# The sample loop of a hybrid decoder step: the copies are queued behind the values' windows, one of them much later, the next sample's third row is formed earlier, and the softmax is divided after the value product

## The chip, the cores and the metric

One core of a Trainium2 chip runs the whole program. The metric is the device time of one execution in microseconds (us). Engines are named as the profile names them: PE is TensorE (matmul), DVE is VectorE, ACT is ScalarE, POOL is GpSimd, SP is SyncE. SP computes nothing here; it only issues transfers (DMAs).

## The reference, cut to what matters

The program is one inference step of a one-layer decoder for a prompt of 256 tokens and eight samples of 4 new tokens each, with 2048 past positions in each sample's cache. For the change only the samples' part of the first attention counts:

```
# per sample b: 4 queries t, 8 heads h, keys at distances 0, d, 2d.. <= window, for (128,1), (512,4), (2048,16)
logits = einsum('bthd,btjhd->bhtj', q, kg) + bias      # gathered keys
lse    = logsumexp(logits); p = exp(logits - lse)
o      = einsum('bhtj,btjhd->bthd', p, vg)             # merged over the three branches by their sums
...
k_win_sample = k_all[:, n_new:]; v_win_sample = v_all[:, n_new:]   # the caches, moved on by 4 rows
```

The last line means that 2044 of 2048 rows of both caches of each sample are copied from input to output: 8 x 2 caches, each in two pieces of 2044 KB, so 32 copies. They depend on nothing. After the attention follow the output projection, cross-attention over 256 memory tokens, a router and a mixture of 32 experts whose 12 MB of weights each are read once, all in float32.

## The kernel before, in words

All loads and the 32 copies are issued by SP in one written order, and their packets are served in that order. A copy (`copy(n)`, L491, `COPIES`, L276) moves memory to memory and is placed wherever the order has room for it.

**Stages.** (1) Projection of all tokens; the weights `w_in` come in eight chunks (L1505). (2) The sample loop, `b` = 1 to 7 (L1204 on DVE, L1704 on PE, L876 on ACT, L547 on SP). (3) The output projection `out` (L1642, L1628). (4) Cross-attention, which starts with the product `xq` (L1749) and its weights `w_xq`. (5) Router and experts (L1954, L1983), where each expert's weights are loaded as soon as the half before has been used.

**One turn of the sample loop.** The key window of sample b (`window(kwin..)`, 1.75 MB in four transfers, two buffers) must be there; ACT copies its late rows together (`late_keys`, L790, L787). PE spreads each of the four query rows over a bank (`row`, L1564); DVE multiplies it with the keys and sums (`row`, L1163), adds biases and finds the largest score (`largest_score`, semaphore `scored`). POOL reduces that over partitions; in the next turn DVE subtracts (`shift`, L1134), ACT exponentiates (`sample_exp`), DVE and POOL form the sums over all keys (`sums`, L1143; L687), DVE divides (`shares`, L1147), and only then PE multiplies with the values (`values`, L1671). This product also waits for the value window (one buffer) and for `late_values` (L797). DVE masks the product (`keep`, L1153), PE turns it (`turn_values`, L1687) and ACT stores it (`sample_out`, L861). Beside this each turn carries one unit of the prompt's attention (`logits`, `share`, `turned`, `unit_values`) and long products of 16 matmuls (`fill`, L1648): `mk` twice in turns 1 and 2, with `w_xk`; `mv` once in turns 3 to 6, with `w_xv`.

**What sets the order.** PE's products rotate over seven banks in the order of `jobs` (L254 to L341): `take` waits until the product seven places before has been read. SP's order in a turn (L547 to L558): wait for `scored` b, key window b+1, then `w_xv` (turn 3), `w_out` (turn 7) or copies, then wait until the value product b-1 is full (L1682 is its last matmul), value window b. A transfer behind such a wait is not issued before it ends.

Of the kernel before, what the change touches and what calls it, by code (L numbers as in the profile page):

```python
# [8 lines left out]
P = 128  # L9
# [43 lines left out]
def constants():  # L53
# [22 lines left out]
    col = np.arange(AW)  # L76
    own = ((p[:, None] // 32 == p[:, None] // 8 % 4) & (p[:, None] % 8 == col[None, :] // HD)).astype(np.float32)
    diag = np.concatenate([own, (p[:, None] // 32 == np.arange(DEC_T)[None, :]).astype(np.float32)], 1)
# [20 lines left out]
def build(nc, i, o):  # L99
# [5 lines left out]
    with ctx:  # L105
# [86 lines left out]
        zs = small[:, 320:352]  # L192
        zz = small[:, 352:384]
        stat = small[:, 384:440]

        own = hn[:, 2, 0:AW + DEC_T]
# [79 lines left out]
        COPIES = [5, 1, 3, 1, 2, 2, 2, 2, 2, 2, 3, 2, 1, 3]  # L276
# [30 lines left out]

        add("pt", DEC_B - 1)
        add("pvt", DEC_B - 2), add("o", DEC_B - 1), add("out", 0, 0), add("out", 0, 1), add("pv", DEC_B - 1)
# [99 lines left out]
        zpart = sem("zpart")  # L409
        zall = sem("zall")  # L410
        prob = sem("prob")
# [56 lines left out]

        block = ctx.enter_context(nc.Block())
# [3 lines left out]
        def _(sp):  # L473
            load(sp, "ident", ident[:, :], i["c_ident"])
            for t in (0, 2, 1):
# [71 lines left out]
            for b in range(1, DEC_B):  # L547
# [105 lines left out]
        def _(pool):  # L653
# [23 lines left out]
            for b in range(DEC_B):  # L677
# [8 lines left out]
                pool.wait_ge(zpart, b + 1)  # L686
                nc.gpsimd.partition_all_reduce(zz, zs, P, bass.bass_isa.ReduceOp.add).then_inc(zall, 1)  # L687
# [60 lines left out]
        def _(act):  # L748
# [12 lines left out]

            act.wait_ge(consts, 2)
# [97 lines left out]

            def sample_out(b):  # L861
# [14 lines left out]
            for b in range(1, DEC_B):  # L876
                unit_pt(b - 1)
                if b >= 2:
                    sample_out(b - 2)
# [4 lines left out]
                unit_out(b - 1)  # L884
                unit_exp(b)
# [4 lines left out]
            unit_pt(DEC_B - 1)  # L890
            sample_out(DEC_B - 2)
            unit_out(DEC_B - 1)
            late_values(DEC_B - 1)
            sample_exp(DEC_B - 1)
# [3 lines left out]
            for t, (t0, n) in enumerate(TOK):  # L898
                if t == 1:
                    sample_out(DEC_B - 1)  # L900
# [109 lines left out]
        def _(dve):  # L1010
# [132 lines left out]
            def sums(b):  # L1143
                dve.wait_ge(sexp, b + 1)
                V.tensor_reduce(zs, pr[:, :, :, :].rearrange("p k t h -> p (t h) k"), AX.X, ALU.add).then_inc(zpart, 1)

            def shares(b):  # L1147
                dve.wait_ge(zall, b + 1)
                link(V.reciprocal(zz, zz))
                V.tensor_tensor(pr[:, :, :, :].rearrange("p k t h -> p k (t h)"), pr[:, :, :, :].rearrange("p k t h -> p k (t h)"),  # L1150
                                zz.unsqueeze(1).broadcast_to([P, 4, 32]), ALU.mult).then_inc(prob, 1)

            def keep(b):  # L1153

                if b:
                    b_, use = place(("pvt", b - 1))
                    dve.wait_ge(bank_full[b_], use + 1)
                else:
                    dve.wait_ge(loaded["diag"], 16)
                ps, s = product(dve, "pv", b)  # L1160
                V.tensor_tensor(kept, ps[:, :], own[:, 0:AW], ALU.mult).then_inc(s, 1)

            def row(b, t):  # L1163
# [3 lines left out]
                if b:  # L1167
                    pair = kw[:, 0:8, :].rearrange("p (k s) n -> p k s n", k=2)[:, :, t, :]
                    V.tensor_tensor(pd[:, 0:2, :], pair, ps[:, :].unsqueeze(1).broadcast_to([P, 2, AW]), ALU.mult)  # L1169
                    V.tensor_tensor(pd[:, 2, :], kw[:, 8, :], ps[:, :], ALU.mult).then_inc(s, 1)  # L1170
                else:
                    V.tensor_tensor(pd[:, 0, :], near_first[:, t, :], ps[:, :], ALU.mult)
                    V.tensor_tensor(pd[:, 1, :], far_first[:, t, :], ps[:, :], ALU.mult)
                    V.tensor_tensor(pd[:, 2, :], late_first, ps[:, :], ALU.mult).then_inc(s, 1)
# [17 lines left out]
            dve.wait_ge(late_k, 1)  # L1192
# [8 lines left out]
            dve.wait_ge(late_k, 2)  # L1201
            row(1, 0), shift(0)
            logits(0)
            for b in range(1, DEC_B):  # L1204
# [4 lines left out]
                dve.wait_ge(late_k, b + 1)  # L1209
                for t in range(0 if b > 1 else 1, DEC_T):  # L1210
# [13 lines left out]
            shift(DEC_B - 1), keep(DEC_B - 2), sums(DEC_B - 1), shares(DEC_B - 1)  # L1224
# [25 lines left out]
            for t, (t0, n) in enumerate(TOK):  # L1250
                residual("out", t)
                if t == 0:
                    keep(DEC_B - 1)
# [208 lines left out]
        def _(pe):  # L1462
# [28 lines left out]
            pe.wait_ge(rb_rep, 1)  # L1491
            for kind in range(6):
# [5 lines left out]
            ps, s = take(pe, "toep")  # L1498
            M(ps[0:HEADS, 0:TOEP], rb, cb[:, 0:TOEP], start=True, stop=True).then_inc(s, 1)
# [171 lines left out]
            def values(b):  # L1671
                pe.wait_ge(prob, b + 1)
# [365 lines left out]
```

## Time and profile before

| | |
|---|---|
| median of 3 runs | 1409.87 us (1401.8 to 1410.43) |
| the profiled execution | 1409.75 us, span 1408.0 us |
| PE busy, DVE busy, ACT busy | 1255.7 us (89%), 481.2 us (34%), 230.3 us (16%) |
| moved by DMA | 557.14 MB, mean 396 GB/s |
| chain that ended last | DMA 55%, PE 35%, DVE 5%, ACT 2% |
| largest piece of the chain | DMA wide<-in_w_gate_up, 49% |

The page cuts the span into 40 slices and gives for each the busy share of every engine in tenths. The chain follows the last instruction back through whatever released it. The rows below come from it and from closer questions: busy time by stretch, the order of instructions of one engine in time, and the chain piece by piece. In a timeline, the bracket gives the idle time before the instruction and what ended it.

### The profile page before, as it was taken

To read this page: it belongs to the slowest core of one execution; us is meant where nothing else is said; L and a number is where in the kernel's file an instruction comes from. 1 tells how busy PE (TensorE), PEld (TensorE's weight loads), DVE (VectorE), ACT (ScalarE), POOL (GpSimd) and SP (SyncE) were. 2 spreads that over 40 slices of the span, in tenths; PEclk is the share of its full clock that TensorE was granted. 3 is DMA by queue.
4 is the path that set the end of the run, shared out by engine and by line. 5 is a ranking of instruction groups with operands and counts; after the bars stand their busy time and mean duration, and the time that the engine had idled before them with its cause. 6 is when DMAs were issued, how large, how long until landed. Compare 5 with 4: busy or idle time off the path is not lost.

```text
span 1408.0 us, 16530 instructions
## 1 busy us (share of the span) xinstructions
PE 1255.7 (89%) x6407; PEld 528.5 (38%) x6407; DVE 481.2 (34%) x1037; ACT 230.3 (16%) x448; POOL 67.7 (5%) x69
## 2 busy tenths in 40 slices
PE   7989877989897999998999989999899998999986
PEld 5444323456644433333333333333333333333332
DVE  2387888332326412312232122321223212132124
ACT  1334443211311110110110100110011010011102
POOL 2010000005007000000000000000000000000000
PEclk9999988999997999999999999999999999999998
DMA  9999999998989699999999999999999999999993
GB/s 339 353 381 363 399 397 379 361 370 306 360 354 344 254 431 427 427 429 426 429 428 429 429 429 429 428 430 427 430 427 430 427 429 428 429 429 429 429 428 158
DMA packets 51740, 557.14 MB, mean 396 GB/s; under 512 B 7021, under 2 KB 9301, under 8 KB 15885
## 3 DMA queue, kind: packets, MB, share of 16 engines
q1 hardware_dynamic: 50629, 553.04, 96.0%
q0 software_dynamic: 1072, 3.57, 0.6%
q8 instruction: 26, 0.43, 0.1%
q14 instruction: 13, 0.11, 0.0%
HBM read 552.02 MB, written 71.72 MB: 443 GB/s over the span
## 4 chain that ended last, share of the span: by engine, by line
DMA 55%; PE 35%; DVE 5%; ACT 2%; issue 1%; SPq 1%; DVEq 0%; ACTq 0%; PEldq 0%
DMA wide<-in_w_gate_up 49%; PE bank L1954 12%; DMA wide<-in_cache_v_win 3%; PE bank L1642 3%; PE bank L1983 2%; PE bank L1684 2%; PE bank L1749 2%; PE bank L1512 2%; PE bank L1508 1%; PE bank L1662 1%; DMA slim<-in_w_xq 1%; DMA slim<-in_w_xv 1%; ACT wide L787 1%; PE bank L1737 1%; PE bank L1791 1%
## 5 line engine op out<-in xcount | busy, mean ns | idle before, releaser
L1954 PE MATMUL bank<-wide,att 128*64 128x512 f32 x2048 | 463.3, 596 | 58.5 <-DMA wide<-in_w_gate_up 58.3
L1954 PEld LDWEIGHTS bank<-wide,att 128*64 128x64 f32 x2048 | 139.3, 136 | 362.5 <-issue 228.8
L1983 PE MATMUL bank<-slim,att 128*64 128x512 f32 x1024 | 226.8, 595 | 0.0
L1422 DVE TENSOR_SCALAR att<-bank 128x512 f32<-128x512 f32 x32 | 22.1, 691 | 469.0 <-PE bank L1954 469.0
L1983 PEld LDWEIGHTS bank<-slim,att 128*64 128x64 f32 x1024 | 70.6, 137 | 152.2 <-issue 149.2
L1401 DVE TENSOR_TENSOR x<-x,bank 128x512 f32<-128x512 f32 x68 | 46.6, 685 | 233.1 <-PE bank L1936 226.4
L980 ACT ACTIVATE att<-att 128x512 f32<-128x512 f32 x32 | 20.2, 630 | 517.6 <-DVE att L1422 517.6
L1936 PE MATMUL bank<-tb,att 128*128 128x512 f32 (+1 forms) x192 | 84.7, 611 | 1.8 <-ACT tb L989 1.3
L989 ACT ACTIVATE tb<-bank 64x512 f32<-64x512 f32 x64 | 37.8, 591 | 234.1 <-PE bank L1983 233.7
L1662 PE MATMUL bank<-slim,ta 128*128 128x512 f32 x128 | 57.8, 601 | 0.5 <-DMA slim<-in_w_xv 0.3
L1176 DVE TENSOR_REDUCE small<-wide 128x24 f32<-128x1536 f32 x28 | 49.1, 1753 | 1.0
L1684 PE MATMUL bank<-wide,pr 128*32 128x512 f32 x192 | 33.0, 840 | 17.5 <-ACT wide L787 11.4
L1903 PE MATMUL bank<-att,mkT 128*128 128x128 bf16 x408 | 46.3, 223 | 1.4 <-DVE att L1352 1.4
L1903 PE MATMUL bank<-att,ta 128*128 128x128 bf16 x408 | 45.7, 222 | 0.0
L787 ACT ACTIVATE wide<-wide 32x512 f32<-32x512 f32 x60 | 37.6, 626 | 44.3 <-DMA wide<-in_cache_v_win 24.5
L1169 DVE TENSOR_TENSOR wide<-wide,bank 128x1024 f32<-128x1024 f32 x28 | 33.9, 1210 | 6.0 <-PE bank L1568 3.9
L1662 PEld LDWEIGHTS bank<-slim,ta 128*128 128x128 f32 x128 | 23.4, 190 | 33.4 <-issue 29.7
L1903 PEld LDWEIGHTS bank<-att,mkT 128*128 128x128 bf16 x408 | 28.3, 99 | 15.2 <-issue 14.6
L1749 PE MATMUL bank<-ta,slim 128*128 128x288 f32 x128 | 31.6, 408 | 2.7 <-DMA slim<-in_w_xq 1.8
L1429 DVE TENSOR_TENSOR att<-att 128x512 f32<-128x512 f32 x32 | 33.4, 1044 | 1.1
L985 ACT ACTIVATE att<-bank 128x512 f32<-128x512 f32 x32 | 19.1, 597 | 74.9 <-PE bank L1974 74.9
L1974 PE MATMUL bank<-ident,att 128*128 128x128 f32 x128 | 21.0, 286 | 11.5 <-DVE att L1429 9.6
(290 smaller groups left out, 1153.1 us busy)
## 6 DMA issues: line engine op xcount, KB each, us to landing
wide<-in_w_gate_up SPq DMA_DIRECT2D x128, 2048.0 KB, 25.4
slim<-in_w_down SPq DMA_DIRECT2D x64, 2048.0 KB, 22.0
out_k_win_sample<-in_cache_k_win SPq DMA_DIRECT2D x16, 2044.0 KB, 25.3
out_v_win_sample<-in_cache_v_win SPq DMA_DIRECT2D x16, 2044.0 KB, 22.9
wide<-in_w_in SPq DMA_DIRECT2D x8, 1024.0 KB, 15.8
wide<-in_cache_v_win SPq DMA_DIRECT2D x8, 1024.0 KB, 7.5
wide<-in_cache_mem_k SPq DMA_DIRECT2D x8, 1024.0 KB, 24.4
wide<-in_cache_mem_v SPq DMA_DIRECT2D x8, 1024.0 KB, 14.7
```

The lines of the kernel that those rows point to most:

```text
L787: ins = A(late[32 * s:32 * s + 32, :], win[96:128, s, :], ACT.Copy)
L989: ins = A(ye[i // 2][CAP * (i % 2):CAP * (i % 2) + CAP, 512 * h:512 * h + 512], bank_y[CAP * h:CAP * h + CAP, :], ACT.Copy)
L1176: link(V.tensor_reduce(S_[b % 2][:, :, t, :], pd.rearrange("p k (h d) -> p k h d", d=HD), AX.X, ALU.add))
L1401: ins = V.tensor_tensor(dst, dst, bk[:, :], ALU.add)
L1642: ins = M(tk[h][0][0:n, :], left[:, k, t0:t0 + n], slim[:, k, 512 * h:512 * h + 512], start=k == 0, stop=k == KC - 1)
L1662: ins = M(ps[:, :], ta[:, k, P * t:P * t + P], slim[:, k, 512 * h:512 * h + 512], start=k == 0, stop=k == KC - 1)
L1684: ins = M(ps[g, :], flat[:, kind, :], vwin[:, 8 if kind == 2 else 4 * kind + t, :], start=k == 0, stop=False)
L1749: ins = M(ps[:, 0:T], slim[:, k, P * c:P * c + P], ta[:, k, :], start=k == 0, stop=k == KC - 1)
L1903: M(bk[:, c:c + 2 * CAP], hparts[t][:, s, P * k:P * k + P], onehot[:, t, :], start=t == 0 and s == 0, stop=False)
L1936: ins = M(out, back[buf][:, t0:t0 + m], ye[buf][:, 512 * h:512 * h + 512], start=True, stop=True)
L1954: ins = M(bk[half[h], :], rows[:, k, :], wide[:, k, c:c + 512], start=False, stop=k == KC - 1)
L1983: ins = M(bank_y[half[h], :], aT[:, f % 4, f // 4, :], slim[:, f, 512 * h:512 * h + 512], start=f == 0, stop=f == KC - 1)
```

## The change

- SP: `COPIES` has 4 instead of 5 copies in front, 2 instead of 1 before the router's late loads, 2 instead of 3 behind expert 0's first weights, and so 2 instead of 1 remain for the end of that place. In the sample loop the copies of a turn are issued behind the value window instead of ahead of it.
- `ident` and the prompt's second tile are loaded from ACT's queue; the 0/1 matrix `own` has 32 columns instead of 516. PE forms the product `toep` ahead of the ten small bias products.
- `row(b + 1, 2)` moves on PE from the start of turn b+1 to just behind `values(b - 1)`, ahead of the long product; `turn_values(b - 2)` moves behind `unit_values`.
- DVE's `sums` and `shares`, POOL's second reduce and the semaphores `zpart`, `zall`, `prob` go. `values` multiplies the undivided exponentials, and 16 matmuls of one column give the sums per row; DVE inverts them (`part_of_sum`), ACT divides while it reads the product (`keep`, now on ACT). The masking falls to `turn_values`, which has 8 matmuls instead of 4.
- DVE waits for the late keys only at the third product of row 0, PE for the late values only at their matmuls.

```
-        COPIES = [5, 1, 3, 1, 2, 2, 2, 2, 2, 2, 3, 2, 1, 3]
+        COPIES = [4, 1, 3, 1, 2, 2, 2, 2, 2, 2, 3, 2, 2, 2]
...
-            add("qb", b, 2), add("pt", b - 1)
+            if b == 1:
+                add("qb", b, 2)
+            add("pt", b - 1)
+            for f in FILL[b, 0]:
+                add(*f)
+            add("qb", b, 3), add("o", b - 1)
             if b >= 2:
                 add("pvt", b - 2)
-            for f in FILL[b, 0]:
-                add(*f)
-            add("qb", b, 3), add("o", b - 1), add("s", b, 0), add("s", b, 1)
+            add("s", b, 0), add("s", b, 1)
             if b + 1 < DEC_B:
                 add("qb", b + 1, 0), add("qb", b + 1, 1)
             add("pv", b - 1)
+            if b + 1 < DEC_B:
+                add("qb", b + 1, 2)
...
                 if b in ROUND_AT:
                     slim_round(ROUND_AT[b])
-                else:
-                    copy(COPIES.pop(0))
 
                 bb, use = place(("pv", b - 1))
                 sp.wait_ge(bank_full[bb], use + 1)
                 window(vwin, i["cache_v_win"], b, v_in)
+                if b not in ROUND_AT:
+                    copy(COPIES.pop(0))
...
+            load(act, "ident", ident[:, :], ident_rows)
+            load(act, "x1", x[:, 1, :], second_rows)
...
+            def keep(b):
+                if b:
+                    b_, use = place(("pvt", b - 1))
+                    act.wait_ge(bank_full[b_], use + 1)
+                act.wait_ge(rz_in, b + 1)
+                ps, s = product(act, "pv", b)
+                A(kept, ps[:, :], ACT.Copy, scale=rz[:, b:b + 1]).then_inc(s, 1)
...
                 unit_pt(b - 1)
                 if b >= 2:
-                    sample_out(b - 2)
+                    keep(b - 2)
                 sample_exp(b - 1)
                 late_values(b - 1)
...
                 unit_out(b - 1)
+                if b >= 2:
+                    sample_out(b - 2)
...
+            def part_of_sum(b):
+
+                b_, use = place(("pv", b))
+                dve.wait_ge(bank_full[b_], use + 1)
+                V.reciprocal(rz[:, b:b + 1], sx_bank[:, b:b + 1]).then_inc(rz_in, 1)
...
-                    if t < 3:
-                        (shift, sums, shares)[t](b - 1)
-                    if b >= 2 and t == 0:
-                        keep(b - 2)
+                    if t == 0 and b > 1:
+                        shift(b - 1)
+                        part_of_sum(b - 2)
...
             def values(b):
-                pe.wait_ge(prob, b + 1)
+                pe.wait_ge(sexp, b + 1)
+                pe.wait_ge(rz_in, b)
                 pe.wait_ge(v_in, 64 * (b + 1))
-                pe.wait_ge(late_v, b + 1)
...
-                for k, kind in enumerate((2, 0, 1, 3)):
+                for kind in range(4):
+                    for t in range(DEC_T):
+                        n = NS if kind == 3 else P
+                        M(sx_bank[32 * t:32 * t + 32, b:b + 1], flat[0:n, kind, :], ones[0:n, 0:1], start=kind == 0, stop=kind == 3,
+                          tile_position=(0, 32 * t))
+                for k, kind in enumerate((0, 1, 2, 3)):
+                    if kind == 2:
+                        pe.wait_ge(late_v, b + 1)
```

## Rows read from the trace of the kernel before

**Rows 1.** The page, 40 slices of 35.2 us: share of the DMA engines, what they moved.
```profile
DMA  9999999998989699999999999999999999999993
GB/s 339 353 381 363 399 397 379 361 370 306 360 354 344 254 431 427 427 429 426 429 428 429 429 429 429 428 430 427 430 427 430 427 429 428 429 429 429 429 428 158
```
**Rows 2.** Busy time by stretch: length, PE, PEld, DVE, ACT, POOL, PEclk, DMA share, GB/s.
```profile
121.00:146.00 25.00, 20.95 (x83) 9.48 (x86) 20.03 (x34) 8.54 (x19) 1.39 (x3) 0.88 1.00 365
190.00:252.00 62.00, 47.77 (x228) 20.11 (x226) 54.67 (x82) 20.94 (x47) 2.89 (x6) 0.83 0.96 368
...
250.00:252.00 2.00, 2.00 (x20) 1.04 (x16) 1.40 (x4) 0.00 (x0) 0.14 (x1) 1.00 0.09 35
...
386.00:399.00 13.00, 12.35 (x99) 6.89 (x99) 2.77 (x4) 1.15 (x3) 0.00 (x0) 0.88 0.68 262
...
454.00:469.00 15.00, 11.15 (x89) 7.52 (x90) 8.80 (x50) 0.95 (x6) 0.00 (x0) 0.77 0.16 54
...
507.00:1360.00 853.00, 786.74 (x4117) 282.82 (x4117) 204.34 (x450) 86.25 (x140) 0.00 (x0) 1.00 1.01 428
```
**Rows 3.** SP's queue in order of time, sample loop: start, duration, transfer.
```profile
120.42 0.33 SPq L512 DMA_DIRECT2D wide<-in_cache_v_win  x1
...
148.23 0.34 SPq L512 DMA_DIRECT2D wide<-in_cache_v_win  x1
...
188.85 0.33 SPq L512 DMA_DIRECT2D wide<-in_cache_v_win  x1
...
209.73 0.33 SPq L512 DMA_DIRECT2D wide<-in_cache_v_win  x1
...
251.24 0.33 SPq L512 DMA_DIRECT2D wide<-in_cache_v_win  x1
```
**Rows 4.** ACT in order of time: the copies of late rows that start with a window's landing.
```profile
138.73 2.54 ACT L787 ACTIVATE wide<-wide 32x512 f32<-32x512 f32 x4 [8.98 <-DMA wide<-in_cache_v_win]
200.89 2.54 ACT L787 ACTIVATE wide<-wide 32x512 f32<-32x512 f32 x4 [3.16 <-DMA wide<-in_cache_v_win]
205.20 2.54 ACT L787 ACTIVATE wide<-wide 32x512 f32<-32x512 f32 x4 [0.32 <-DMA wide<-in_cache_k_win]
221.75 2.54 ACT L787 ACTIVATE wide<-wide 32x512 f32<-32x512 f32 x4 [2.70 <-DMA wide<-in_cache_v_win]
...
258.57 2.54 ACT L787 ACTIVATE wide<-wide 32x512 f32<-32x512 f32 x4 [4.53 <-DMA wide<-in_cache_v_win]
```
**Rows 5.** PE in order of time, front: the second tile's transposes, the first projection matmuls.
```profile
9.53 1.97 PE L1486 MATMUL bank<-ident,x 128*128 128x128 f32 x8 [2.55 <-DMA x<-in_x_prompt]
...
17.72 4.18 PE L1508 MATMUL bank<-ta,wide 128*128 128x288 f32 x8 [0.77 <-ACT att L775]
```
**Rows 6.** DVE in order of time, turn 6: first product of row 0, `keep`, `sums`.
```profile
208.84 1.21 DVE L1169 TENSOR_TENSOR wide<-wide,bank 128x1024 f32<-128x1024 f32 x1
...
213.03 0.69 DVE L1161 TENSOR_TENSOR wide<-bank,hn 128x512 f32<-128x512 f32 x1 [0.21 <-DVE pp L1139]
...
219.15 0.38 DVE L1145 TENSOR_REDUCE small<-pr 128x32 f32<-128x128 f32 x1 [1.92 <-ACT pr L859]
```
**Rows 7.** PE in order of time: small products, a long product, value products, first of `xq`.
```profile
71.25 0.84 PE L1560 MATMUL bank<-att 64*32 64x32 f32 x16 [1.51 <-ACT att L805]
...
120.29 7.13 PE L1662 MATMUL bank<-slim,ta 128*128 128x512 f32 x16
...
203.68 4.99 PE L1684 MATMUL bank<-wide,pr 128*32 128x512 f32 x24 [3.09 <-ACT wide L787]
...
268.03 2.78 PE L1684 MATMUL bank<-wide,pr 128*32 128x512 f32 x24
...
302.29 1.71 PE L1749 MATMUL bank<-ta,slim 128*128 128x288 f32 x6 [0.90 <-DVE ta L1046]
```
**Rows 8.** The chain that ended last, in order of time: start, duration, what.
```profile
158.53 14.80 DMA slim<-in_w_xv
...
290.67 15.09 DMA slim<-in_w_xq
```

More of the change, by code:

```diff
@@ L191, in build @@
         gm = small[:, 288:320]
-        zs = small[:, 320:352]
-        zz = small[:, 352:384]
+        rz = small[:, 320:320 + DEC_B]
         stat = small[:, 384:440]
-        own = hn[:, 2, 0:AW + DEC_T]
+        own = hn[:, 2, 0:HEADS * DEC_T]
         kept = wf[:, 15360:15872]
@@ L473, in _ @@
         def _(sp):
-            load(sp, "ident", ident[:, :], i["c_ident"])
-            for t in (0, 2, 1):
+            for t in (0, 2):
                 t0, n = TOK[t]
@@ L890, in _ @@
             unit_pt(DEC_B - 1)
+            unit_out(DEC_B - 1)
+            keep(DEC_B - 2)
+            sample_exp(DEC_B - 1)
+            late_values(DEC_B - 1)
             sample_out(DEC_B - 2)
-            unit_out(DEC_B - 1)
-            late_values(DEC_B - 1)
-            sample_exp(DEC_B - 1)
             act.wait_ge(stored["mk"], 16)
@@ L899, in _ @@
                 if t == 1:
+                    keep(DEC_B - 1)
                     sample_out(DEC_B - 1)
@@ L1141, in shift @@
                 dve.sem_inc(shifted, 1)
[L1143 to L1161, printed above, removed]
+            def part_of_sum(b):
+                b_, use = place(("pv", b))
+                dve.wait_ge(bank_full[b_], use + 1)
+                V.reciprocal(rz[:, b:b + 1], sx_bank[:, b:b + 1]).then_inc(rz_in, 1)
             def row(b, t):
@@ L1223, in _ @@
             share(DEC_B - 1, DEC_B, P * (UNITS[DEC_B - 1][1] + 1))
-            shift(DEC_B - 1), keep(DEC_B - 2), sums(DEC_B - 1), shares(DEC_B - 1)
+            shift(DEC_B - 1), part_of_sum(DEC_B - 2)
             for u in range(2):
@@ L1252, in _ @@
                 if t == 0:
-                    keep(DEC_B - 1)
+                    part_of_sum(DEC_B - 1)
                 norm(5 + t, n, x[0:n, t, :], hn[0:n, t, :], 6 + t)
@@ L1491, in _ @@
             pe.wait_ge(rb_rep, 1)
+            ps, s = take(pe, "toep")
+            M(ps[0:HEADS, 0:TOEP], rb, cb[:, 0:TOEP], start=True, stop=True).then_inc(s, 1)
             for kind in range(6):
@@ L1690, in turn_values @@
                 ps, s = take(pe, "pvt", b)
-                for c in range(4):
-                    ins = M(ps[:, 4 * c:4 * c + 4], kept[:, P * c:P * c + P], own[:, AW:AW + DEC_T], start=True, stop=True)
+                if b == 0:
+                    pe.wait_ge(loaded["diag"], 16)
+                for h in range(HEADS):
+                    ins = M(ps[64 * (h % 2):64 * (h % 2) + 64, 4 * (h // 2):4 * (h // 2) + 4], kept[:, HD * h:HD * h + HD],
+                            own[:, DEC_T * h:DEC_T * h + DEC_T], start=True, stop=True)
                 ins.then_inc(s, 1)
@@ L1704, in _ @@
             for b in range(1, DEC_B):
-                row(b, 2)
+                if b == 1:
+                    row(b, 2)
                 turned(b - 1)
-                if b >= 2:
-                    turn_values(b - 2)
                 for f in FILL[b, 0]:
@@ L1712, in _ @@
                 unit_values(b - 1)
+                if b >= 2:
+                    turn_values(b - 2)
                 scores(b)
@@ L1716, in _ @@
                 values(b - 1)
+                if b + 1 < DEC_B:
+                    row(b + 1, 2)
                 for f in FILL[b, 1]:
@@ L1719, in _ @@
             turned(DEC_B - 1)
-            turn_values(DEC_B - 2)
             unit_values(DEC_B - 1)
@@ L1724, in _ @@
             rows_times("out", 0, tb, P, 0)
+            turn_values(DEC_B - 2)
             values(DEC_B - 1)
```

23 lines of the change are left out of this document (9 added, 14 removed).

## The prediction

> **What bounds the kernel now.** I read the slices of the page first: the DMA engines are busy in nearly every slice [rows 1]. By stretch they are full in turns 1 and 2 of the sample loop, nearly full in the later turns and all through the experts [rows 2]; the idle spots are 250 to 252 us, 386 to 399 (0.32 x 13 = 4.2 us) and 454 to 469 (0.84 x 15 = 12.6 us). So up to the weights of `xq` the end is set by bytes in SP's order plus whatever time that queue stands empty. SP's order next [rows 3]: value windows are issued at 120.42, 148.23, 188.85, 209.73 and 251.24; the 20.9 us from the third to the fourth are one steady turn. Landings are read from ACT [rows 4]. The last window met an empty queue and landed after 258.57 - 251.24 = 7.3 us. A window alone takes 205.20 - 200.89 = 4.3 us, so about 3.0 us are issue and completion. Between 205.20 and 221.75 lie one window and two copies: a **copy** costs (16.55 - 4.3) / 2 = 6.1 us. A turn of two windows and two copies is 20.8 us, which is the turn seen: the loop runs at the pace of the queue. Value window 1 landed after 18.3 us, so 11.0 us of other work lay ahead of it. That backlog is what kept the queue full while PE did the two long products of turn 2.
>
> **The change, part by part.**
>
> *Front.* PE waited 2.55 us for the second tile and 0.77 us for ACT's copy of `toep` [rows 5]; the new loads and the new order attack both. Bounds 0 and 3.3; I take 2.5, since other loads (gains, bias) are due at about the same time. PE's front then leads by 2.5 us. The Trainium skill (DMA: Bandwidth & Descriptors, section Issuing engines are not separate DMA queues) says that starting a transfer from another engine saves only the time to start it; by that rule the tile would gain about 1 us and the front 1.8.
>
> *Softmax divided late.* Gone from DVE per turn: the wait ahead of `sums` (1.92), `sums` (0.3 net), `shares` (two small operations, about 0.6 by the size of `sums`) and `keep` (0.6 and a gap of 0.2) [rows 6]; added a reciprocal (0.2). DVE's turn falls by 3.3 us from the 20.9 of the queue that it follows; worth nothing as long as the queue sets the pace. Gone from POOL one reduction, hidden. Added on PE 16 matmuls, 32 records, of 32 columns of weights and one of data. Not in the trace: bounds 0 (beside others) and 3.8 us (long weights); the nearest row is 16 small records in 0.84 us [rows 7], or 52 ns each, 1.7 us; I take 2.0, twice that at the low clock. The Trainium skill (TensorE: Matmul & The Clock Gate, section LDWEIGHTS) lets the load time follow the number of columns alone; its 27 ns for 32 columns would make an estimate of 0.9 us. `turn_values` with 16 records instead of 8: 0 to 0.8 us, hidden by PE's slack in turns 4 to 6. `keep` on ACT (0.7) stands ahead of `sample_exp` and `late_values`, and it waits for `part_of_sum` on DVE, behind row 0; PE's `turn_values` and scores wait for it. PE is ahead of DVE there, so 0.
>
> *Banks.* With the third row and `turn_values` moved, the bank of `values(b - 1)` is the one of `row(b, 3)`, seven places before. So the value product can't start before DVE has multiplied row 3: row 0 and `shift` 4.2 us, rows 1 and 2 at 3.5 each (219.15 - 1.92 - 213.72), and by the 1.21 of a product of two thirds about 1.9 for row 3's products and 1.3 for `logits`, together 14.4 us after DVE's turn began [rows 6]. That is what `prob` cost before, so the wait is replaced, not removed. The third row ahead of the long product takes 0.3 us from it and hides nothing, as DVE reaches row 2 later than either place. The late waits save 1.2 us on DVE and about 2 on PE, hidden in the same way.
>
> *Copies, place by place.* One copy fewer in front and turn 1's one behind value window 1: 12.2 us fewer ahead of it against 11.0 us of backlog. The queue reaches it empty.
>
> Gap A. Value window 1 is issued near 120 (front -2.5, new matmuls +2.0). Then come 4.3 + 6.1 + 4.3 = 14.7 us of work (window, copy, key window 3), and SP stands at its wait for value product 1. PE needs two long products (14.1), the row sums (2.0), the product (2.8 and 1.0) and some eight small groups like the one of 0.84, less what lies side by side, an estimate of 5.5: 25.5; before, the interval was 27.8. Empty for 11 us (9 to 13).
>
> Value window 2 is then issued at 145.5. Ahead of the end of `w_xv` lie the window 4.3, two copies 12.2, key window 4.3 and `w_xv` itself, 4.19 MB at the 428 GB/s of the experts [rows 2], 9.8; with 3.0 for completion it lands at 179.1, against 158.53 + 14.80 = 173.3 before [rows 8]. `mv` waits for it.
>
> Gap B. From that landing to the next value window's issue passed 188.85 - 173.3 = 15.5 us, filled by two windows and copies. Now only the two windows (8.6) are issued before that wait, as turn 3 has no copies. Empty for 15.5 + 3.0 - 8.6 = 10, less the store of `mem_k` (2.5) which falls here or just before; I take 7 (5 to 10).
>
> Gap C. Value window 4 goes out at 194.6, then two copies, then key window 6, which lands at 194.6 + 4.3 + 12.2 + 4.3 + 3.0 = 218.4. DVE's turn 6 begins there; it began at 208.84 before. Value product 5 starts 1.4 (late keys) + 14.4 later and takes 5.8 to 8, so it is full at 240 to 242, while the queue ran out after 4.3 + 12.2 + 4.3 of turn 5, at 237. Empty for 4 (0 to 9). What was late before was the value window; what is late now is the **key window behind two copies**.
>
> *The end of it.* Empty time 11 + 7 + 4 = 22 us; before, 250 to 252 cost 1.8 and its edges 0.5. One copy fewer ahead of `w_xq` is -6.1. So `w_xq` lands 22 - 2.3 - 6.1 = **13.6 us later**. PE was ready for `xq` at 302.29 [rows 7] and went on at 290.67 + 15.09 = 305.8: 3.5 us of cover, and PE's own path moves by less than the weights do, so all 13.6 count. From there to the experts PE and DVE set the pace, and the shift is carried.
>
> *The late copies.* Two copies instead of one after 386: 6.1 us into 4.2 of idle, so expert 0's weights come 2 us later; they are first used when the router is done, near the end of the idle stretch 454 to 469, and that leaves them slack. The one moved behind `w_down` goes into those 12.6 us; if that idle time were used up, expert 1's weights would start later by the overflow, at most 1 us. 0.
>
> **Sum.** 1409.75 (the profiled execution, next to the median 1409.87) + 13.6 = **1423 us**. With the low ends of the gaps (14) it is +5.6, with the high ends (32) +23.6.
>
> **Rivals.**
> 1. *The queue stays fed; the moved copy is the gain.* If the value product is full much sooner (PE never waits, its clock stays up) the gaps A and C shrink to the 2.3 us there were, and gap B disappears behind the store and early issue. Then the copy taken to 386 us is worth 6.1 and the gap at 250 another 2.3: 1401.4. It decides if the gaps sum to under 8.4 us. For it: DVE loses 3.3 us a turn and PE's waits for `late_values` go. Against it: gap A stands on two long products that nothing shortens.
> 2. *The clock falls at each value product.* A value product after 3.09 us of idle PE took 4.99 us, one right behind other matmuls 2.78 [rows 7], and PEclk was 0.83 in these turns against 1.00 later. With more waiting in turns 2, 3, 5 and 6 each adds 1.5 us for the sums and 1 for the product: +10 on the chain, 1433. The Trainium skill (TensorE: Matmul & The Clock Gate, section HAM oscillation) says that a matrix engine which waits for transfers restarts at 1.2 GHz; the trace agrees.
> 3. *Nothing on balance.* The gaps come to 8 to 13 us because stores and the order hide part: 1408 to 1414.
>
> **How the numbers follow.** The forecast case (+6 to +19) has 0.50, rival 1 0.13, rival 2 0.20, rival 3 0.17. About 1% (14 us) is what can be told from no change here. Slower by more than that: 0.22 of the forecast case, all of rival 2: 0.42. Faster by more: only a tail of rival 1, 0.03. The rest is 0.55. The range runs from rival 1 to just over rival 2, 1402 to 1435.
>
> **What would show it.** Right: value window 1 lands within 8 us of its issue; the DMA share falls well under 1.00 between 135 and 146 and again behind `w_xv`; `w_xv` lands near 179; ACT's copy for key window 6 starts near 218; `w_xq` lands near 319; DVE's turns wait for key windows. Wrong: a DMA share of 1.00 through 121 to 146, or a loop turn of under 20 us with both windows early. If `w_xq` comes later but the experts start no later, the carrying was wrong.

## The result, and the profile after

| | before | after |
|---|---|---|
| median, same chip and hour | 1408.09 us (1401.8 to 1410.43, 4 runs) | 1431.49 us (1429.98 to 1432.42, 4 runs) |
| ratio | 1 | 1.0178, 95% interval 1.0149 to 1.0207 |
| profiled execution, span | 1409.75, 1408.0 | 1429.98, 1428.2 |
| chain: DMA, PE | 55%, 35% | 54%, 36% |

The change costs 23.4 us by the medians and 25 by the ratio. The forecast was 1423 in a range of 1402 to 1435, a change of 13.6: the direction, the place and the mechanism are right, the size is about 10 us short. The measured time lies nearer to the 1433 of rival 2 than to 1423; why that rival is not the cause stands below, with the other rivals.

The page of after, cut into 40 slices like [rows 1]: the digits 8, 7 and 8 in the fourth, sixth and seventh slice of the DMA line are holes that were not there.

```profile
DMA  9998978999999799999999999999999999999993
GB/s 354 347 358 291 338 278 309 382 377 365 334 324 395 304 402 427 428 427 426 430 427 428 430 427 430 429 427 429 429 427 431 427 427 430 428 427 431 427 427 161
```

After by stretch; the last three numbers are the granted clock, the share of the DMA engines and GB/s, as in [rows 2]. The first row reaches from 83 us, near the first key window of the turns, to where `xq` gets its last weights.

```profile
83.00:328.40 245.40, 198.27 (x1159) 89.92 (x1158) 146.85 (x227) 83.85 (x184) 8.02 (x14) 0.85 0.89 336
121.00:146.00 25.00, 22.66 (x136) 9.93 (x135) 21.00 (x30) 9.10 (x19) 1.28 (x2) 0.93 0.60 236
146.00:190.00 44.00, 31.68 (x182) 13.90 (x180) 25.56 (x36) 14.41 (x30) 1.01 (x2) 0.81 0.99 381
190.00:200.00 10.00, 7.96 (x67) 2.38 (x68) 9.62 (x16) 4.04 (x11) 0.43 (x1) 0.66 0.02 6
190.00:252.00 62.00, 48.08 (x308) 19.15 (x309) 44.35 (x64) 20.53 (x47) 1.30 (x3) 0.78 0.75 276
```

The same stretch in the kernel before:

```profile
83.00:305.80 222.80, 187.62 (x847) 85.97 (x845) 160.87 (x254) 79.02 (x176) 11.71 (x22) 0.92 0.99 381
```

Length times (1 - share) gives the time without transfers: 245.4 x 0.11 = 27.0 us after, 222.8 x 0.01 = 2.2 before (each 1.2 either way, as the share has two digits). Length times share is the time with them: 218.4 and 220.6. So the whole of the 22.6 us by which `xq` is later is time in which the transfer engines stood still: 24.8 us more of it, and 2.2 less of transfers.

SP's queue after (answers to [rows 3]): the first key window of the turns (83.26 before), value windows 1 and 2, the weights `w_xv`, value window 4 with the two copies and the key window that now follow it, and value window 6:

```profile
80.09 0.33 SPq L513 DMA_DIRECT2D wide<-in_cache_k_win  x1
...
119.69 0.33 SPq L513 DMA_DIRECT2D wide<-in_cache_v_win  x1
...
145.10 0.33 SPq L513 DMA_DIRECT2D wide<-in_cache_v_win  x1
...
152.26 15.35 SPq L509 DMA_DIRECT2D slim<-in_w_xv  x8
...
199.10 0.33 SPq L513 DMA_DIRECT2D wide<-in_cache_v_win  x1
...
201.29 0.63 SPq L495 DMA_DIRECT2D out_v_win_sample<-in_cache_v_win  x1
201.96 0.60 SPq L495 DMA_DIRECT2D out_k_win_sample<-in_cache_k_win  x1
202.60 0.60 SPq L513 DMA_DIRECT2D wide<-in_cache_k_win  x1
...
247.25 0.33 SPq L513 DMA_DIRECT2D wide<-in_cache_v_win  x1
```

ACT after, at the start of turn 6 ([rows 4] before), and DVE there ([rows 6] before): both wait for the key window that stands behind two copies.

```profile
224.80 2.54 ACT L788 ACTIVATE wide<-wide 32x512 f32<-32x512 f32 x4 [12.74 <-DMA wide<-in_cache_k_win]
```

```profile
224.80 1.22 DVE L1168 TENSOR_TENSOR wide<-wide,bank 128x1024 f32<-128x1024 f32 x1 [8.97 <-DMA wide<-in_cache_k_win]
```

PE after ([rows 7] before): row sums (L1680) and value product (L1690) of turns 2, 4 and 7, between them the long product that waited for `w_xv`, and `xq`. L1171 is the second instruction of a row's product on DVE, over the last third of its key rows:

```profile
139.10 0.54 PE L1680 MATMUL bank<-ones,pr 128*32 128x1 f32 x32 [2.34 <-DVE wide L1171]
139.57 4.48 PE L1690 MATMUL bank<-wide,pr 128*32 128x512 f32 x24
...
173.05 5.91 PE L1661 MATMUL bank<-slim,ta 128*128 128x512 f32 x8 [7.31 <-DMA slim<-in_w_xv]
...
192.04 0.71 PE L1680 MATMUL bank<-ones,pr 128*32 128x1 f32 x32 [2.34 <-DVE wide L1171]
192.68 5.35 PE L1690 MATMUL bank<-wide,pr 128*32 128x512 f32 x24
...
257.21 0.54 PE L1680 MATMUL bank<-ones,pr 128*32 128x1 f32 x32
257.68 2.78 PE L1690 MATMUL bank<-wide,pr 128*32 128x512 f32 x24
...
328.40 11.79 PE L1761 MATMUL bank<-ta,slim 128*128 128x288 f32 x35 [1.23 <-DMA slim<-in_w_xq]
```

The chain after, its transfers up to `xq` ([rows 8] before). A key window is on it now.

```profile
162.54 20.84 DMA slim<-in_w_xv
...
204.57 20.21 DMA wide<-in_cache_k_win
...
267.44 18.68 DMA wide<-in_cache_v_win
...
309.46 18.90 DMA slim<-in_w_xq
```

From `xq` to the experts the shift is carried almost whole: 22.6 us there, 19.75 at the first weights of expert 1 (issued at 467.00 before, 486.75 after), 20.2 in the span.

### The profile page after: what moved, and what is told of

Read it like the earlier page. It is cut to its first block, busy times and chain, and to the rows that moved or that the text cites. A ratio compares the mean times of both kernels' runs of the same rounds, so it can differ in the third digit from the quotient of the medians.

```text
span 1428.2 us, 17140 instructions
## 1 busy us (share of the span) xinstructions
PE 1268.1 (89%) x6727; PEld 533.1 (37%) x6727; DVE 469.4 (33%) x1013; ACT 235.2 (16%) x456; POOL 64.3 (5%) x61
## 4 chain that ended last, share of the span: by engine, by line
DMA 54%; PE 36%; DVE 6%; SPq 2%; issue 1%; ACT 1%; DVEq 0%; PEldq 0%; ACTq 0%
DMA wide<-in_w_gate_up 48%; PE bank L1966 12%; PE bank L1661 2%; PE bank L1995 2%; PE bank L1761 2%; PE bank L1641 2%; PE bank L1690 2%; PE bank L1511 1%; DMA slim<-in_w_xv 1%; PE bank L1573 1%; DMA wide<-in_cache_k_win 1%; DMA slim<-in_w_xq 1%; DMA wide<-in_cache_v_win 1%; PE bank L1507 1%; PE bank L1749 1%
## 5 line engine op out<-in xcount | busy, mean ns | idle before, releaser
L993 ACT ACTIVATE att<-att 128x512 f32<-128x512 f32 x32 | 20.2, 631 | 517.9 <-DVE att L1421 517.9
L1761 PE MATMUL bank<-ta,slim 128*128 128x288 f32 x128 | 36.8, 451 | 5.7 <-DMA slim<-in_w_xq 5.7
L1690 PE MATMUL bank<-wide,pr 128*32 128x512 f32 x192 | 33.8, 855 | 0.0
L1761 PEld LDWEIGHTS bank<-ta,slim 128*128 128x128 f32 x128 | 26.6, 211 | 15.6 <-DMA slim<-in_w_xq 5.9
## 6 DMA issues: line engine op xcount, KB each, us to landing
wide<-in_w_gate_up SPq DMA_DIRECT2D x128, 2048.0 KB, 25.5
```

Of the source, the lines that this page charges most:

```text
L1690: ins = M(ps[g, :], flat[:, kind, :], vwin[:, 8 if kind == 2 else 4 * kind + t, :], start=k == 0, stop=False)
L1761: ins = M(ps[:, 0:T], slim[:, k, P * c:P * c + P], ta[:, k, :], start=k == 0, stop=k == KC - 1)
```

## The experiments

Two theories at the start. **S**: SP's order is the cause; with the copies behind the value window, nothing is left to transfer while SP waits for the value product. **C**: the order of the computation is, with a value product that waits for the third row and meets a low clock. Each time below is a median with the kernel before run beside it on the same chip; that kernel gave 1405.5, 1407.1 and 1406.7 us in the three sets, single runs from 1399.9 to 1413.7. One profiled execution therefore stands up to 7 us off its median, and differences of a few us are read from the medians. Profiles of kernels with the same front differ before any of the moved work is reached: in the nine profiles with the whole new front PE begins the first projection product between 12.49 and 15.48 us (14.92 after; 12.65, 12.49 and 12.83 in experiments 1, 6 and 8). Some 2 us of a difference between two `xq` times can be that. "`xq` goes at" is the time at which PE had its last weights or operands for `xq` in the profile (305.8 before, 328.4 after).

**1. Copies ahead again.** In the changed kernel:

```
                 if b in ROUND_AT:
                     slim_round(ROUND_AT[b])
+                else:
+                    copy(COPIES.pop(0))
                 bb, use = place(("pv", b - 1))
                 sp.wait_ge(bank_full[bb], use + 1)
                 window(vwin, i["cache_v_win"], b, v_in)
-                if b not in ROUND_AT:
-                    copy(COPIES.pop(0))
```

> The changed kernel with one part undone: in the sample loop the copies stand ahead of the value window again, as in the kernel before; everything else of the change stays. Theory S (the order on SyncE's queue costs it: with the copies behind the values the transfer engines stand empty for about 10, 10 and 4.5 us at 136, 190 and 244 us): the empty stretches go, the weights w_xq land 6 to 9 us ahead of the kernel before (which landed them at 307.0), and the time is 1400 to 1406 us. Theory C (the order of the computation costs it: each value product is held by DVE's product of the third row of the next sample, and runs at the low clock): the time stays at 1420 us or more.

1402.63 us (10 runs), ratio to before 0.9988 (0.9961 to 1.0015); `xq` goes at 297.8. By stretch:

```profile
83.00:297.80 214.80, 186.81 (x1153) 85.98 (x1151) 143.94 (x225) 83.41 (x184) 7.46 (x14) 0.90 1.00 379
121.00:146.00 25.00, 21.57 (x131) 9.19 (x130) 19.98 (x31) 8.76 (x19) 0.43 (x1) 0.86 0.98 373
190.00:200.00 10.00, 6.60 (x76) 3.39 (x78) 7.92 (x11) 5.95 (x15) 0.00 (x0) 0.82 1.03 428
```

One part undone takes back the whole loss, 27 us by the ratios and 29 by the medians, and the holes with it: 0.60 becomes 0.98, 0.02 becomes 1.03. Theory C falls: the clock was 0.86 in these 25 us, lower than the 0.93 after, and it did not matter.

**2. The counts alone.** Changed kernel, `COPIES` of before (five in front), copies behind.

```
-        COPIES = [4, 1, 3, 1, 2, 2, 2, 2, 2, 2, 3, 2, 2, 2]
+        COPIES = [5, 1, 3, 1, 2, 2, 2, 2, 2, 2, 3, 2, 1, 3]
```

> The changed kernel with only the counts of the copies of before (five at the front and one in the last place, for four and two); the copies stay behind the values. Theory S: the fifth copy at the front is moved out of full stretches only, so 0 to 3 us come back or are lost: 1426 to 1433 us. If the count mattered more than the order, the time would fall to 1415 us or less.

1434.85 us (4 runs), ratio 1.0218 (1.0173 to 1.0262); `xq` goes at 330.7. The time is 1.9 us above what was expected at most. Moving one copy away from the front gave the changed kernel 2.3 us at `xq`, 3.4 by the medians and 5.6 by the ratios. The two intervals overlap, so this doesn't tell the 6.1 of the forecast from less.

**3. The order alone.** Kernel before, and in it:

```
                     slim_round(ROUND_AT[b])
-                else:
-                    copy(COPIES.pop(0))
...
                 window(vwin, i["cache_v_win"], b, v_in)
+                if b not in ROUND_AT:
+                    copy(COPIES.pop(0))
```

> The kernel before with one part of the change alone: in the sample loop each copy stands behind the value window. Softmax, row order, counts and front are those of before. Theory S: the time rises by 12 to 19 us, to 1420 to 1427 us, with empty stretches of the transfer engines ahead of value windows 2, 4 and 6. Theory C: at most 1411 us.

1427.61 us (4 runs), 0.6 above the expected range, ratio 1.0148 (1.0106 to 1.0191); `xq` goes at 320.2.

```profile
83.00:320.20 237.20, 194.29 (x845) 86.34 (x843) 160.24 (x253) 79.34 (x176) 11.76 (x22) 0.89 0.94 356
121.00:146.00 25.00, 25.00 (x106) 11.21 (x105) 22.28 (x35) 8.65 (x19) 1.39 (x3) 1.00 0.83 311
190.00:200.00 10.00, 10.00 (x40) 3.55 (x33) 9.54 (x15) 2.14 (x4) 0.43 (x1) 0.93 0.55 206
```

A move of one statement, with not a byte and not an instruction more, makes 21 of the 25 us (by the ratios 0.0148 and 0.0178) of the whole change. It does so at a granted clock of 1.00 in the stretch with the first hole, so a slow PE is no condition for it.

**4. The old queue under the new computation.** Changed kernel, the edit of experiment 1 and

```
-        COPIES = [4, 1, 3, 1, 2, 2, 2, 2, 2, 2, 3, 2, 2, 2]
+        COPIES = [5, 1, 3, 1, 2, 2, 2, 2, 2, 2, 3, 2, 1, 3]
```

> The changed kernel with SyncE's order and counts of the sample loop both as before; softmax divided late, the third row early, and the first loads on ACT stay. Theory S: within 3 us of the kernel before, 1405 to 1411 us. Theory C: 1420 us or more. Beside the first kernel of this set it gives what the one copy moved from the front is worth: some 4 us against it, if full stretches carry a moved copy one for one.

1406.65 us (10 runs), ratio 0.9992 (0.9969 to 1.0014); `xq` goes at 299.9. Against experiment 1 the moved copy shows 4.0 us by the medians, but 0.6 by the ratios, and the single runs of both reach from 1398 to 1407.5 and more; the 2.1 us at `xq` are no more than the 1.9 by which this profile began its first projection product later (14.56 for 12.65). So its worth is not shown here. Late division, early third row and new front together are worth nothing that can be told at the end.

**5. The third row back.** Changed kernel, in the list of PE's work:

```
-            if b == 1:
-                add("qb", b, 2)
-            add("pt", b - 1)
+            add("qb", b, 2), add("pt", b - 1)
...
-            if b + 1 < DEC_B:
-                add("qb", b + 1, 2)
```

> The changed kernel with one part undone: the product of row 2 of the next sample stands ahead of the scores' transposition again, as before; copies stay behind the values. Forecast's step on the gate (the value product waits until DVE has taken row 3 out of the bank, whichever row stands first, because the same banks turn round): if the early third row is what makes the value windows 1, 2 and 4 late, the empty stretches shrink to those of the kernel with only the order changed (share of the transfer engines .83 at 121:146) and xq is let go at about 320 us instead of 328; time 1423 to 1428 us. If it is the late division that makes them late, nothing moves: 1430 to 1434 us, xq at 326 to 330.

1433.47 us (2 runs), ratio 1.0191 (1.0147 to 1.0235); `xq` goes at 327.0, 121:146 has a share of 0.61. Nothing moves beyond the noise, so the early third row is not what makes the holes longer than in experiment 3.

**6. One copy ahead, one behind.** Changed kernel, where turn 1 has its only copy ahead:

```
                     slim_round(ROUND_AT[b])
+                else:
+                    copy(1)
+                    COPIES[0] -= 1
```

> The changed kernel with one copy of each turn ahead of the value window and the other behind it. A copy occupies the transfer engines for some 6 us. Theory S: each gap is filled by 6 us of its 10, 10 and 4.5, so xq is let go at 309 to 314 us (328.4 after, 297.8 with all copies ahead) and the time is 1411 to 1417 us. If the loss were all or nothing (one late value window shifts all that follows), it stays above 1423 us.

1411.09 us (8 runs), ratio 1.0025 (1.0008 to 1.0043); `xq` goes at 308.1, 0.9 us below the expected range.

```profile
83.00:308.10 225.10, 191.67 (x1153) 87.03 (x1151) 144.59 (x225) 83.48 (x184) 7.46 (x14) 0.88 0.95 362
121.00:146.00 25.00, 21.75 (x131) 9.19 (x130) 20.02 (x31) 8.77 (x19) 0.43 (x1) 0.86 0.78 298
190.00:200.00 10.00, 9.68 (x38) 3.83 (x30) 9.50 (x11) 0.94 (x3) 0.00 (x0) 0.99 0.72 278
```

The price is graded: `xq` at 328.4, 308.1, 297.8 with none, one or all of a turn's copies ahead, and 0.11, 0.05 and 0.00 of the stretch without transfers. The first copy brings back 20 us (of which some 2 may be the earlier start of this profile) and the second 10, as the first fills 6 us of each hole and the holes were only 10, 10 and 4 long. It is bytes in the hole that count, not whether a window is late.

**7. Two copies from ahead of `w_xq` to the end.** Experiment 1 with

```
-        COPIES = [4, 1, 3, 1, 2, 2, 2, 2, 2, 2, 3, 2, 2, 2]
+        COPIES = [4, 1, 3, 1, 2, 2, 2, 2, 2, 0, 3, 2, 2, 2]
```

> The kernel with all copies ahead of the values (first of the set before) with two copies more taken from the place just ahead of the weights w_xq and put last, behind step 0 of the experts, where the transfer engines stand empty for about 10 us ahead of step 1 in every kernel of this study. If the time is set by how full the transfer engines are up to step 1, w_xq lands some 8 us earlier (289 to 291 us), the last copies cost nothing, and the time is 1390 to 1396 us. Rival: the chain through the computation from xq to the experts is not shortened, or the two copies delay step 1 by their 12 us; then it stays at 1400 to 1406 us.

1400.68 us (10 runs), ratio to before 0.9966 (0.9941 to 0.9991): the rival of the expectation. The weights are no longer what `xq` waits for; DVE is:

```profile
295.62 9.69 PE L1761 MATMUL bank<-ta,slim 128*128 128x288 f32 x32 [2.24 <-DVE ta L1059]
```

So `xq` goes 2.2 us earlier than in experiment 1 instead of 8 (about 4 if the 1.9 us by which this profile began later are taken off), and 34 x 0.23 = 7.8 of the 12 us of transfers moved away became a hole in the place they left, where experiment 1 has a share of 1.00:

```profile
252.00:286.00 34.00, 33.38 (x198) 14.70 (x197) 8.06 (x22) 7.73 (x14) 0.00 (x0) 1.00 0.77 298
```

**8. Turns without copies.** Changed kernel with

```
-        COPIES = [4, 1, 3, 1, 2, 2, 2, 2, 2, 2, 3, 2, 2, 2]
+        COPIES = [4, 1, 3, 0, 0, 0, 0, 0, 0, 0, 3, 2, 2, 2]
```

All 32 copies are still made, 15 of them behind step 0.

> The changed kernel with all 13 copies of the turns and of the place ahead of w_xq moved behind step 0. No copy stands ahead of or behind a value window, so what is left is what the turns take by their computation and windows alone. Theory S: value window b is then issued when its product lets it, w_xq is let go at 275 to 285 us, and a turn is near 20 us. Theory C (the order of the computation is itself slower): w_xq is not let go before 300 us. The time itself is worse for the 13 copies now standing in one place: 13 x 6.1 = 79 us, less 10 to 15 of empty time, less what the turns gain (15 to 25 against the kernel before): 1440 to 1465 us.

1473.77 us (1 run). SP's value windows 3, 4, 5 and 6:

```profile
163.32 0.33 SPq L513 DMA_DIRECT2D wide<-in_cache_v_win  x1
...
184.19 0.33 SPq L513 DMA_DIRECT2D wide<-in_cache_v_win  x1
...
204.27 0.33 SPq L513 DMA_DIRECT2D wide<-in_cache_v_win  x1
...
224.44 0.33 SPq L513 DMA_DIRECT2D wide<-in_cache_v_win  x1
```

With no copies in the queue the turns from value window 4 on take 20.1 and 20.2 us. Experiment 1, the same computation with two copies a turn ahead of the wait, issues these windows at 184.80, 204.86 and 225.03: 20.1 and 20.2 as well. So the copies were free there, and the computation alone sets this pace. Against the 20.9 of [rows 3] in the kernel before that is at most 0.8 us a turn for DVE's relief, and none of it shows in the time (experiment 4). `w_xq` was issued at 282.6, inside the 275 to 285 expected, but `xq` went only at 297.0, as DVE's operand was not ready: the earlier weights gained nothing. The time is 9 us above my range for the same reason, and because a copy costs more than 6.1 us: 75.3 us more than the execution of experiment 1 (1398.46), plus some 10 us that stood empty there at 440 to 456, is 85 us for 13 copies, an estimate of 6.6 each.

**9. Order and the two loads.** The edits of experiments 3 and 10 in the kernel before, of which the second is

```
+            load(act, "ident", ident[:, :], ident_rows)
+            load(act, "x1", x[:, 1, :], second_rows)
```

> The kernel before with two parts of the change: the copies behind the value windows, and the identity matrix and the second rows of the prompt loaded from ACT's queue. Division, row order and counts are those of before. With the order alone xq was let go at 320 us, with the late division and this front besides at 327. If the late division is what makes up the difference, this kernel lets xq go at 316 to 320 us and takes 1422 to 1428 us. If the earlier start of the windows only makes the empty stretch behind them longer and shifts the rest, it lets xq go at 324 us or later: 1430 us or more.

1430.14 us (4 runs), ratio 1.0175 (1.0156 to 1.0195); `xq` goes at 321.7, between the two theories. The median is 2.5 us above experiment 3 and 4.7 below experiment 2 (which has the late division and the new PE order besides, with the same five copies in front). With intervals of this width the times only say that neither part is large. The traces say more of the first hole. With the two loads the share of 121:146 falls from 0.83 to 0.67: the earlier front makes the hole longer. And from value window 1 to value window 2 pass 21.4 us here and in experiment 3, but 25.2 to 26.7 in after and experiments 2 and 5, the kernels that have the late division and the copies behind.

**10. The two loads alone.** Kernel before with them.

```
-            load(sp, "ident", ident[:, :], i["c_ident"])
-            for t in (0, 2, 1):
+            for t in (0, 2):
...
+            load(act, "ident", ident[:, :], ident_rows)
+            load(act, "x1", x[:, 1, :], second_rows)
```

> The kernel before with the new front alone (the identity matrix and the second rows loaded from ACT's queue). Forecast's step: the first key window of the turns is issued some 3 us earlier (80.1 against 83.3 us) and, the transfer engines being full from there to w_xq, all of it reaches the end: 2.5 us less than the kernel before, ratio .998. Rival: it is lost on the way, ratio 1.000.

1404.00 us (12 runs), ratio 0.9982 (0.9966 to 0.9997), 2.5 us by the ratio (0.4 to 4.8): as forecast. `xq` goes at 302.1, 3.7 us earlier than before. Where the queue is fed, a front that is earlier comes through; behind a hole (experiment 9 against 3) it does not.

**11. Copies ahead and the third row back.** The edits of experiments 1 and 5 in the changed kernel, of which the second is

```
-            if b == 1:
-                add("qb", b, 2)
-            add("pt", b - 1)
+            add("qb", b, 2), add("pt", b - 1)
```

> The kernel with all copies ahead of the values, with the product of row 2 back in its old place, so only the late division, the front and the counts of the change are left. Forecast's step: the early third row hides nothing, so the same time as with it: 1400 to 1406 us, ratio to that kernel within .3%. If the early third row is worth what fills TensorE's wait ahead of the long product (3.1 us a turn before), xq starts 6 us or more later.

1402.03 us (10 runs), ratio 0.9971 (0.9954 to 0.9988), against 1402.63 with the early third row. No worth of it can be told, with the holes or without.

**12. Kernel before, two copies last.**

```
-        COPIES = [5, 1, 3, 1, 2, 2, 2, 2, 2, 2, 3, 2, 1, 3]
+        COPIES = [5, 1, 3, 1, 2, 2, 2, 2, 2, 0, 3, 2, 1, 3]
```

> The kernel before with the two copies that stand just ahead of w_xq put last, behind step 0 of the experts, and nothing else. Before, xq waited for w_xq from 290.7 to 305.8 us while 456 to 467 us stood empty. w_xq is then bound by its own issue (287.9 us) and its transfer: landed at 298 to 300 us, 6 to 8 us earlier, and the last copies fit into the empty stretch: 1398 to 1402 us, ratio .993 to .996. Rival: as with the two copies last in the kernel with the late division (1400.7 for 1402.6), nearly nothing comes through: ratio .998 or above.

1403.12 us (12 runs), ratio 0.9978 (0.9967 to 0.9989). Half of what was expected:

```profile
302.17 31.28 PE L1749 MATMUL bank<-ta,slim 128*128 128x288 f32 x128 [0.87 <-DVE ta L1046]
```

`xq` goes at 302.2 for 305.8. The forecast had read the cover right (3.5 us, from PE ready at 302.29 in [rows 7]), and I did not use it here: of weights that come about 8 us earlier only those 3.5 count.

## Why the forecast was right, and where it was short

*Copies, the decisive step: right.* "What was late before was the value window; what is late now is the key window behind two copies": DVE waited 8.97 us for key window 6. (It waited 9.56 for key window 4 too, at 171.70, which the forecast left out; there `w_xv` came later still and set the time.) Experiments 1 and 3, each one statement, switch the loss off and on. Value window 2 was forecast at 145.5 and issued at 145.10.

*The three holes.* Read from after:

| | forecast | after |
|---|---|---|
| A | 11 (9 to 13) | 25.00 x 0.40 = 10.0 |
| B | 7 (5 to 10) | 10.00 x 0.98 = 9.8 |
| C | 4 (0 to 9) | 244 to 250: 6 x 0.71 = 4.3 |
| elsewhere | 0 | 27.0 less these three: 2.9 (1.2 either way) |

*Gap A: right in the sum, by luck in the parts.* From value window 1 to 2 the forecast had 25.5 us and the trace has 25.4. But it had 5.5 for the small groups and 2.0 for the row sums, where the trace has some 3.3 and 0.5; and it had no wait and a value product at full clock, where PE waited 2.34 us for DVE and the product took 4.48 instead of 2.78. This wait is the one that the forecast called replaced; in experiment 3, with the old division, PE had none there and the product at 137.86 took 2.78. So with the copies behind, the late division, with the order on PE that comes with it, costs 4.0 us of this interval (21.4 in experiments 3 and 9).

**Gap B** was put too small. The forecast took 2.5 us off for the store of `mem_k`, "which falls here or just before". It fell before: between 144 and 185 us the trace of after has 14.80 MB, 1.05 of them this store. POOL issued it at 161.98 us; in the kernel before, where the turn's second reduce stood ahead of it on POOL, at 178.86, and in experiment 9 at 185.09. So it filled no hole and stood ahead of `w_xv`, which PE had at 183.4 instead of the forecast's 179.1, and value window 4 followed at 199.10 for 194.6. In experiment 9, with the store behind that stretch, `w_xv` was there at 179.6. The store can explain 2.5 of the 4.3 us by which `w_xv` was late, an estimate from its bytes; the rest I can't name. From `w_xv` to that value window passed 15.7 us, forecast 15.5.

*Key window 6* landed 25.7 us after value window 4 was issued, forecast 23.8. Two copies at the 6.6 of experiment 8 in place of 6.1 would make 1.0 of it.

*"One copy fewer ahead of `w_xq` is -6.1": right in bytes, not in time; the largest miss.* In the stretch to `xq` 245.4 x 336 = 82.5 MB were moved for 84.9 before, and 2.4 MB are 6.2 us at the rate of before. But the time with transfers fell by only 2.2 us, as the busy engines moved 378 GB/s for 385. The two digits of the share leave 2 GB/s to rounding on either side, so up to 4 of these 7. The lower rate isn't tied to the holes, as experiment 1 had 379 without any; its cause stays open.

Together: empty time +24.8 for +19.7, transfers -2.2 for -6.1, which is 22.6 for 13.6. Of the 9.0 us missing at `xq`, 3.9 are the moved copy, 2.8 gap B and 2.9 the small empty spots outside the three gaps, which the forecast had at nothing (1.0 of them at 83 to 98, a share of 0.93 where before had 1.00); gap A takes 1.0 off.

*Front: right.* PE's wait for the second tile is gone, the first key window of the turns was issued at 80.09 for 83.26, and the loads alone are worth 2.5 us in experiment 10. Over all profiles PE begins the first projection product at 16.93 to 17.72 us with the old front (3 kernels), at 15.54 and 16.04 with the loads alone, and at 12.49 to 15.48 with the whole new front (9 kernels, the middle one 14.56): about 1.5 us for the loads and 2.7 for all, forecast 2.5. The wait of 0.77 us for ACT's copy of `toep` is still there with the loads alone and gone with PE's new order, which no run took by itself; the rest is within the spread of single profiles. By the rule of the Trainium skill (DMA: Bandwidth & Descriptors, Issuing engines are not separate DMA queues) I had about 1 us for the tile and 1.8 for the front, both somewhat below what the profiles show; that only the time to issue is saved, no run here shows or refutes.

*Row sums: too dear.* 32 records in 0.54 us at a granted clock of 1.00 and 0.71 at 0.50, forecast 2.0. The estimate from the Trainium skill (TensorE: Matmul & The Clock Gate, LDWEIGHTS) was 0.9, also too high, but here it was the better guide than the row of 16 small records in 0.84 us.

*Banks: right in place.* PE waits 2.34 us for DVE's L1171 ahead of the row sums in turn 4, 10.8 us in five such waits in all. That the wait only replaces the old one doesn't hold in turn 2 (gap A). No worth of the early third row can be told, as forecast (experiments 5 and 11).

*Late division: "worth nothing as long as the queue sets the pace": right* with the queue fed (experiments 4 and 10: ratios 0.9992 and 0.9982, with overlapping intervals). Experiment 8 adds the reason: the computation alone takes 20.1 us a turn.

*Rival 1* (the queue stays fed, 1401.4) is what experiment 1 built: 1402.6. Its condition, that PE is done early, was not met in the changed kernel. Where the queue was kept fed by other means, `xq` went 8.0 us earlier than before, as its sum had it, but the time fell by only 1.7 us by the ratio (between 5.5 less and 2.1 more); that 1402.6 is close to 1401.4 is in part luck, since the sum starts from the profiled 1409.75 and not from the 1405.5 of that set.

*Rival 2* (the clock, 1433) came nearer to the time than the forecast did, but not by its cause. It has its rows: value products of 5.35 us after a wait and 2.78 without one, where the granted clock was 0.78 over 190 to 252. The low clock does lengthen the holes: the transfer engines stand still until the value product is done, and the products at the end of the three holes took 4.48, 5.35 and 5.10 us, each on the chain. But the rival wanted more of it than before, and there is hardly more: the six products of turns 2 to 7 took 28.0 us after and 27.4 before. The row sums added 0.2 us each at the low clock and not 1.5. And experiment 1 has products of 4.5 to 5.3 us too and loses nothing, as its queue is full meanwhile. The Trainium skill (TensorE: Matmul & The Clock Gate, HAM oscillation) says that PE restarts slow after waiting for transfers; the trace agrees: after 7.31 us of waiting for `w_xv` 8 records of the long product took 5.91 us at a granted clock of 0.62, where 16 take 7.03 at full clock.

*The carrying: right* within 3 us (22.6 at `xq`, 19.75 and 20.2 behind it). *The late copies at 0:* not contradicted; 454 to 490 is busier (0.81 for 0.62), and experiments 7 and 12 put two more there without a loss that could be told.

## What to carry to other kernels

In a queue that is served in order, what stands ahead of a wait is what runs during the wait: put transfers that nobody needs ahead of the issuing engine's wait, and those that somebody needs behind it as early as its condition allows. Price a reordering by the time the queue will stand empty at each wait, and count every store of other queues on both sides of that wait. Before moving work out of a full queue, read what the consumer waits for second: the gain ends at that cover, and the rest becomes a hole.

The lowest time is that of experiment 7, 1400.7 us, 0.34% under the kernel before (0.09 to 0.59%). Its interval overlaps those of experiments 10, 11 and 12, and experiment 12 reaches 0.22% with one number moved, so the computation changes that it carries are not shown to be worth anything.

## What the runs showed of the hardware that was not expected

- A copy from memory to memory of 2044 KB takes the engines 6.1 to 6.6 us (estimates from [rows 4] and experiment 8), or 317 to 343 GB/s, beside 4.3 us for a window of 1792 KB (427 GB/s) [rows 4]. In experiment 8, where 15 copies stand in a row, the engines moved 326 to 340 GB/s in every 10 us from 480 to 520.
- Issuing itself can take long: the eight transfers of `w_xv` took 15.35 us to issue after, with two copies and a key window issued just ahead of them (14.16 in experiment 3, 14.84 in 2), and 3.8 to 3.9 us in experiments 1 and 4, where those copies stand ahead of the value window. What holds SP there no run shows. Value window 3 stood behind them, 2.2 us after its product was done.
- Products of 32 columns of weights and one column of data, which go to four column groups in turn, follow each other at 17 ns a record at a granted clock of 1.00 and 22 ns at 0.50, their weight loads included (32 in 0.54 and 0.71 us).
